# Order of the first weight unit, two products of a cleared tile ahead of it, and the first row sum one unit later

## The reference, cut to what matters

```
u = _rmsnorm(h, g_mix_pre[i])          # y = x * rsqrt(mean(x*x) + EPS) * g
z = u @ w_in[i]
a_b, a_c, a_x, q_lat, kv_lat, k_rope, gate_a, gate_b = jnp.split(z, split_pts, axis=-1)
...
q = (_rmsnorm(q_lat, g_q_lat[i]) @ w_q_up[i]).reshape(bsz, s, N_HEADS, QK_DIM)
kv = (_rmsnorm(kv_lat, g_kv_lat[i]) @ w_kv_up[i]).reshape(bsz, s, N_HEADS, NOPE_DIM + V_DIM)
```

## Time and profile before

| | us |
|---|---|
| median of 3 runs | 1761.85 |
| lowest and highest | 1761.74, 1763.17 |
| the profiled execution | 1760.45 |
| its span in the trace | 1758.7 |
| TensorE busy in it | 1723.8 |
| VectorE, GpSimd, ScalarE busy | 1013.7, 988.5, 630.2 |

### The profile page before, as it was taken

The page is one execution under the profiler, slowest core; times in us unless marked ns, Lnnn a source line. Parts: engine busy times, 40 slices in busy tenths (PEclk is TensorE's granted clock), DMA queues, the critical chain, the costliest instruction groups (busy, mean ns, idle before and its releaser), DMA issues. The chain is left out here.

```text
span 1758.7 us, 22520 instructions
## 1 busy us (share of the span) xinstructions
PE 1723.8 (98%) x8062; PEld 1430.9 (81%) x8062; DVE 1013.7 (58%) x1668; ACT 630.2 (36%) x1182; POOL 988.5 (56%) x586
## 2 busy tenths in 40 slices
PE   7999999999999999998999999999999999999998
PEld 6788788788877888887788888888778888888887
DVE  7778543245661554254678745546657977776244
ACT  4454321243312222043734332332433126766022
POOL 5555566655666666654664556554565663333654
PEclk9999999999999999998999999999999999999999
DMA  5322222222223222322222222222232221111222
GB/s 204 102 73 84 84 96 95 96 85 84 96 96 105 90 100 95 101 96 84 84 84 72 84 72 96 72 84 74 82 103 84 85 96 60 49 49 60 84 85 84
DMA packets 49768, 154.36 MB, mean 88 GB/s; under 512 B 8976, under 2 KB 9104, under 8 KB 49552
## 3 DMA queue, kind: packets, MB, share of 16 engines
q1 hardware_dynamic: 48816, 151.59, 25.7%
q10 hardware_dynamic: 864, 1.57, 0.3%
HBM read 151.05 MB, written 2.10 MB: 87 GB/s over the span
## 5 line engine op out<-in xcount | busy, mean ns | idle before, releaser
L721 POOL TENSOR_SCALAR w_hi<-raw 128x1024 fp32r<-128x1024 f32 (+1 forms) x279 | 299.2, 1072 | 694.1 <-issue 509.6
L723 POOL TENSOR_TENSOR w_lo<-raw,w_hi 128x1024 fp32r<-128x1024 f32 (+1 forms) x279 | 664.8, 2383 | 23.2
L749 PE MATMUL bank<-op_hi,w_hi 128*128 128x512 f32 x984 | 392.0, 398 | 12.1 <-DVE op_lo L2403 8.5
L751 PE MATMUL bank<-op_hi,w_lo 128*128 128x512 f32 x984 | 384.7, 391 | 0.0
L750 PE MATMUL bank<-op_lo,w_hi 128*128 128x512 f32 x984 | 384.7, 391 | 0.0
L749 PE MATMUL bank<-r,w_hi 128*128 128x512 f32 x856 | 340.1, 397 | 4.1 <-POOL w_lo L723 1.4
L751 PE MATMUL bank<-r,w_lo 128*128 128x512 f32 x856 | 334.4, 391 | 0.0
L750 PE MATMUL bank<-r,w_hi 128*128 128x512 f32 x856 | 334.0, 390 | 0.0
L749 PEld LDWEIGHTS bank<-op_hi,w_hi 128*128 128x128 f32 x984 | 185.9, 189 | 52.2 <-ACT fx L1682 8.4
L751 PEld LDWEIGHTS bank<-op_hi,w_lo 128*128 128x128 f32 x984 | 185.6, 189 | 39.3
L750 PEld LDWEIGHTS bank<-op_lo,w_hi 128*128 128x128 f32 x984 | 186.0, 189 | 37.1 <-issue 1.0
(11 more groups left out here) (279 smaller groups left out, 2454.7 us busy)
## 6 DMA issues: line engine op xcount, KB each, us to landing
raw<-in_weights SPq DMA_DIRECT2D x276, 512.0 KB, 3.3
out<-h SPq DMA_DIRECT2D x8, 256.0 KB, 2.0
h<-in_x SPq DMA_DIRECT2D x3, 512.0 KB, 6.9
cst<-in_consts SPq DMA_DIRECT2D x1, 1156.5 KB, 9.8
rope_cos<-in_p ACTq DMA_DIRECT2D x3, 256.0 KB, 3.7
rope_sin<-in_p ACTq DMA_DIRECT2D x3, 256.0 KB, 4.0
h<-in_x SPq DMA_DIRECT2D x2, 256.0 KB, 3.8
rope_cos<-in_positions SPq DMA_DIRECT2D x2, 256.0 KB, 11.9
```

The costliest lines, as they stand in the source:

```text
L721: pool.tensor_scalar(hi, raw[:, r, at:w], 1.0, 0.0, ALU.mult, ALU.add).then_inc(hi_ready, 1)
L723: pool.tensor_tensor(lo, raw[:, r, at:w], hi.bitcast(F32), ALU.subtract).then_inc(split_ready, 1)
L749: pe.matmul(o, ah, bh, start=start, stop=False, skip_group_check=skip)
L751: return pe.matmul(o, al, bh, start=False, stop=stop, skip_group_check=skip)
```

## The change

TensorE: two fp32 products of the tile `fx[:, 3, :]`, which VectorE clears to zero, are put ahead of the first unit. The first unit is written out by hand: all 8 high x high products first (which need `hi_ready`, `hi0` and `hi1`), then the 8 with low weights (`split_ready`), then the 8 with low activations (`lo0`, `lo1`). The first row sum goes from behind the second unit to behind the third. VectorE: one more memset, 128 x 512, behind the one that is there.

```diff
@@ -794,11 +794,29 @@
             a, d, z = enter(pe, "pe", "start")
-            blockwise(U0["lat"], "start", range(2))
+            pe.wait_ge(cleared, 2)
+            for n in range(2):
+                pe.matmul(ps[3][:, :], fx[:, 3, 0:P], fx[:, 3, :], start=True, stop=True)
+            u = U0["lat"]
+            pe.wait_ge(hi_ready, u + 1)
+            for k in range(2):
+                pe.wait_ge(a.sem, a.at(f"hi{k}"))
+                for m in range(4):
+                    pe.matmul(ps[m][:, :], w_hi[:, u % 2, 4 * k + m], op_hi[:, k], start=k == 0, stop=False)
+            pe.wait_ge(split_ready, u + 1)
+            for k in range(2):
+                for m in range(4):
+                    pe.matmul(ps[m][:, :], w_lo[:, u % 2, 4 * k + m], op_hi[:, k], start=False, stop=False)
+            for k in range(2):
+                pe.wait_ge(d.sem, d.at(f"lo{k}"))
+                for m in range(4):
+                    mm = pe.matmul(ps[m][:, :], w_hi[:, u % 2, 4 * k + m], op_lo[:, k], start=False, stop=False)
+            mm.then_inc(unit_done, 1)
+            blockwise(u, "start", range(1, 3))
             pe.wait_ge(cst_in, 16)
             pe.wait_ge(d.sem, d.at("acc7"))
             z.done(full_sum(4), "sum")
-            blockwise(U0["lat"], "start", range(2, 4))
+            blockwise(u, "start", range(3, 4))
 
@@ -2464,6 +2482,7 @@
             clear(st[:, 63:64])
+            clear(fx[:, 3, :])
             dve.wait_ge(gain_in, 16)
             a, d, z = enter(dve, "dve", "start")
```

## The result

The changed kernel takes 1768.88 us (median of 7 runs, 1765.65 to 1769.9) against 1761.74 us for the kernel before in the same comparison (1759.41 to 1763.21): ratio 1.0036, 95% interval 1.0026 to 1.0046. It is slower by 7.1 us where 6.1 were forecast; the interval is 4.6 to 8.1 us.

What follows compares the result with a forecast made beforehand. TensorE, busy 98% of the span, was taken as the bound. The later L773 (+4.0 us) and lost clock (+2.1) sum to +6.1 us, moving the median from 1761.85 to about 1768.0 us; range 1764.8 to 1770.8.

Steps and rivals of the forecast that it cites:

- Step 1: At the start, two zero products take 3.5 us; first real product at 8.9 us, 0.4 later; new order gains nothing.
- Step 2: Clock rises at 9.8 us; TensorE is through the second unit at 20.2 us (19.8 to 21.7), gaining 1.4 us.
- The rival that zeros warm nothing: Zero products at the start don't lift the clock, or it stays low for 10 us: 1769.5 to 1770.5 us; chance 0.13.
- Step 3: Third unit's load lands at 15.9 us, releasing GpSimd's split at 16.2; the unit begins about 20.2, ends at 25.65.
- Step 4: Moved row sum L767 starts at 25.65 us; its 16.5 us chain makes L773 4.0 us later, behind a 6.0 us wait.
- Step 5: Behind the 6.0 us wait TensorE's clock falls to 1.2 GHz, costing 2.1 us (1.6 to 2.8).
- The sum: Whole kernel: +4.0 us for the later L773 plus +2.1 us for the clock, +6.1 us in total.
- The claim that the chain keeps its length: From L767 to L773 it stays 16.5 us, GpSimd's split keeping its distance; bounds: no change or 2.7 us shorter.

Runs made afterwards that it cites:

- e7: Run e6 without the two zero products and their memset; 1762.43 us, ratio to the kernel before 1.0004.
- e8: Run e7 with the third unit's load issued ahead of that of the constants; 1762.21 us, ratio to the kernel before 1.0008.
- e3: Changed kernel plus six useless fp32 products behind the fifth unit's 18 products, ahead of TensorE's wait for `acc2`; 1767.0 us, ratio to the kernel before 1.0032.
- e10: Changed kernel with VectorE's last three angle steps and what hangs on them moved from ahead of `z0` to behind `lo2`; 1761.75 us, ratio 0.9996.
- e1: Kernel before with only the row sum moved behind the third unit, no zero products, old order; 1768.93 us, ratio 1.0043.
- e2: Changed kernel with the row sum put back behind the second unit, zero products and new order kept; 1760.67 us, ratio 0.9994.
- e4: Changed kernel with the row sum one unit later still, behind the fourth unit; 1770.9 us, ratio to the kernel before 1.0056.
- e5: Changed kernel with the row sum inside the third unit, behind 6 of its 24 products; 1768.54 us, ratio to the kernel before 1.0045.
- e6: Run e5 with four of VectorE's angle steps moved ahead of the reciprocal; 1762.09 us, ratio to the kernel before 1.0001.

## Why the prediction was right

- **Step 1** held. The zero products are held by the stage's entry and take 3.5 us of the engine, as forecast. They end at 9.2 instead of 8.9, as the entry itself came 0.27 us later in this execution (5.67). That the new order gains nothing held only because the zeros use up what it gives: e7 and e8 show that it brings the second unit's end about 1 us forward by itself.
- **Step 2** held in kind: the clock rose inside the first eight real products, at 10.66, where 9.8 was forecast. One bound of the step is mis-added: 8.9 + 10.9 + 0.46 x 4.4 is 21.8, not 21.7. The rival that zeros warm nothing falls with e7's rows beside the changed kernel's, and with the times of the rise in all thirteen.
- **Step 3** held for GpSimd (third split from 16.05, released by the DMA, done at 20.17) but it did not set the third unit's start in the changed kernel's execution: the second unit ended last, at 20.83, 0.6 us after the 20.2 forecast: 0.27 us for the later entry, 0.4 for the later rise. L767 is therefore at 26.27, not 25.65. In e3 and e10, where the clock rose at 9.6 and 9.7, the split did decide.
- **Step 4**, the term that decided, held: +4.57 us instead of +4.0, the difference being that of steps 1 and 2, handed on; chain 16.39 against 16.5; the wait, counted as in the prediction from where the next product could have started, 5.96 against 6.0 (the profile's idle of 5.79 counts from the last one's modelled end). e1 shows that the moved sum alone makes it, e2 that without it nothing is lost, e10 that it is the chain behind the sum and not the sum's place as such.
- **Step 5** held, with two gaps. The cost was 2.62 us against 2.1, within 1.6 to 2.8, and e3 shows it by itself. The dense work was slow for about 4 us (44.38 to 48.4), less than the mean of 4.6; what the term left out is L773 itself, whose short products ran at the slow clock too and cost 0.81 us. And the step says that TensorE has two such stands in the trace before. It overlooked a third fall, behind hardly any stand (last section).
- The sum was 6.1 us, measured 7.1; the two terms that were too small by 0.6 and 0.5 us are as large as the difference.
- The claim that the chain keeps its length was right for the reason given, the same place of the split behind the sum. Its bounds were one-sided: I saw that the chain could become 2.7 us shorter (e4 shows 2.8), and missed that it could become 2.7 us longer (e5), because I counted only the steps with two SBUF sources as exposed.

## What to carry to other kernels

Before moving a reduction later to feed TensorE sooner, measure the serial chain that hangs on its result and compare it with TensorE's work up to the next use. Here the chain was 16.5 us against 15.9 us of work, already the longer, and each product moved ahead of the sum lengthened the wait one for one as long as the chain kept its length (e1: 5.4 us more wait for 5.45 us of products). Taking steps that aren't needed yet out of that chain took the loss away without touching TensorE. Then look at what runs beside the chain on the other engines: placed otherwise against GpSimd's splits, the same chain took 13.6 us (e4) to 19.1 us (e5). A wait of TensorE is not paid by its length alone: here the slow clock behind it added more than half as much again, and in e3's trace useless work that ended before the data came kept it off.

## What the runs showed of the hardware that I had not expected

- 1.48 and 1.54 us of idle (e6, e7, e8, e10), followed by the short matmuls of L773, were enough for 3.3 us at the 1.2 GHz level; 0.38 us (before, e2) and 0.65 us (e3) were not. Idle time isn't all of it: in the kernel before the granted clock also fell at 750.25 us, with 0.16 us of idle ahead of sixteen one-column products. Ten of the thirteen profiled executions kept the clock at this same place, so neither figure is a threshold. The row, and the stretches before and behind the fall:

```profile
748.00 1.92 PE L773 MATMUL bank<-cst,fx 128*128 128x1 f32 x16 [0.16 <-ACT fx L1937]
```

```profile
748.00:750.20 2.20, 2.20 (x18) 2.16 (x19) 0.00 (x0) 0.82 (x2) 2.15 (x1) 1.00 0.57 220
750.30:753.60 3.30, 3.30 (x13) 2.83 (x12) 0.14 (x1) 0.60 (x1) 0.00 (x0) 0.50 0.48 159
```

- VectorE's tensor_scalar with a single SBUF source is held up beside GpSimd's split as one with two is: 2.50 us against 0.43 (e5). The reciprocal is not (3.35 us in every run, however much of a split lies beside it), nor are the steps that read one source from PSUM (three of L2397 in 1.89 us in all runs).
- In every trace the difference at the mark is carried to 740 us within 0.3 us. Over the rest of the unchanged program the order of the times did not follow the mark closely: e10 is 2.0 us later at the mark and equal in time, e1 8.9 and 6.8, e5 7.0 and 6.9. Below 3 us the timeline tells more here than five rounds of timing.
